# Two-block transformer on one core: the last four pairs of the second block's gates as seven block products, and the memory's norm and rounding beside the mixing's output product

## The reference, cut to what matters

```python
proj = h @ w_in[l]                      # h: 512 x 1024, the normed stream
q_a, k_a, v_a, u_b, gate_b, gate_c, g_a, g_b = jnp.split(proj, split_points, axis=-1)
...
branch_a = o_a @ w_branch_a[l]          # 512 x 512 @ 512 x 1024
branch_b = y_b @ w_branch_b[l]
merged = jax.nn.sigmoid(g_a) * branch_a + jax.nn.sigmoid(g_b) * branch_b
x = x + merged @ w_mix_out[l]
x = x + memory_cross_attention(rms_norm(x, norm_mem_q[l]), rms_norm(mem, norm_mem_kv[l]),
                               w_mem_q[l], w_mem_kv[l], w_mem_o[l])
```

## Time and profile before

| what | value |
|---|---|
| median of 3 runs | 1548.49 us (1548.48 to 1548.87) |
| profiled execution, its own time | 1548.38 us |
| its span | 1546.6 us |
| granted TensorE clock over the span | 0.999 |
| PE busy | 1536.8 us (99%) |
| VectorE, ScalarE, GpSimd busy | 1055.0, 754.5, 69.1 us |
| DMA | 161.88 MB, mean 105 GB/s |

### The profile page before, as it was taken

One profiled execution on the slowest core, in us unless ns is written; L12 is line 12 of the kernel. 1 busy time (PEld: TensorE's weight loads), 2 busy tenths in 40 slices (PEclk: granted clock), 3 DMA queues, 4 the chain that ended last, 5 costly groups with the idle time before them and its releaser, 6 DMA issues.

```text
span 1546.6 us, 22323 instructions
## 1 busy us (share of the span) xinstructions
PE 1536.8 (99%) x8348; PEld 1330.0 (86%) x8348; DVE 1055.0 (68%) x1755; ACT 754.5 (49%) x1307; POOL 69.1 (4%) x60
## 2 busy tenths in 40 slices
PE   9999999999999999999999999999999999999998
PEld 7888888888899899888888888888888899989987
DVE  6776887768789575447777545555555899948735
ACT  5446677744457445444544334344444445524514
POOL 0000000020000000210000010020002000000002
PEclk9999999999999999999999999999999999999999
DMA  5333222332323233324351242334123333322322
GB/s 195 122 109 97 88 78 93 103 129 90 127 84 110 96 96 108 97 82 131 118 141 62 71 137 87 118 118 156 55 82 109 110 103 110 124 96 82 110 89 75
DMA packets 56235, 161.88 MB, mean 105 GB/s; under 512 B 7232, under 2 KB 8640, under 8 KB 56000
## 3 DMA queue, kind: packets, MB, share of 16 engines
q1 hardware_dynamic: 55504, 159.41, 31.7%
q0 software_dynamic: 320, 0.52, 0.2%
q10 hardware_dynamic: 304, 0.52, 0.1%
HBM read 148.89 MB, written 2.10 MB: 98 GB/s over the span
## 4 chain that ended last, share of the span: by engine, by line
PE 96%; DVE 2%; ACT 1%; issue 1%; DMA 1%; SPq 0%; DVEq 0%; ACTq 0%
PE G L1490 66%; PE TP L1490 10%; PE SC L1490 9%; PE O L1490 5%; PE M L1490 5%; PE TP L1946 1%; PE TP L1892 0%; DMA T<-QK 0%; DVE WL L2623 0%; DMA GN<-in_gains 0%; PE TP L1995 0%; ACT L2030 0%; SPq L1465 0%; ACT WH L2033 0%; DVE T L2917 0%
## 5 line engine op out<-in xcount | busy, mean ns | idle before, releaser
L1490 PE MATMUL G<-XGh,WH 128*128 128x512 f32 x920 | 362.2, 394 | 0.0
L2623 DVE TENSOR_TENSOR WL<-RAW,WH 128x1024 fp32r<-128x1024 f32 (+2 forms) x269 | 282.7, 1055 | 116.5 <-ACT WH L2033 116.2
L1490 PE MATMUL G<-XGh,WL 128*128 128x512 f32 x920 | 358.4, 390 | 0.0
L1490 PE MATMUL G<-XGl,WH 128*128 128x512 f32 x920 | 358.3, 389 | 0.0
L2033 ACT ACTIVATE WH<-RAW 128x1024 fp32r<-128x1024 f32 (+2 forms) x275 | 240.0, 881 | 93.3 <-PE G L1490 60.8
L1490 PEld LDWEIGHTS G<-XGh,WL 128*128 128x128 f32 x920 | 172.7, 188 | 36.5
L1490 PEld LDWEIGHTS G<-XGh,WH 128*128 128x128 f32 x920 | 172.8, 188 | 36.1
L1490 PEld LDWEIGHTS G<-XGl,WH 128*128 128x128 f32 x920 | 172.9, 188 | 34.3 <-DVE XGl L2623 0.2
L1490 PE MATMUL G<-MGh,WH 128*128 128x512 f32 x372 | 145.0, 390 | 0.0
L1490 PE MATMUL G<-MGl,WH 128*128 128x512 f32 x372 | 144.8, 389 | 0.0
L1490 PE MATMUL G<-MGh,WL 128*128 128x512 f32 x372 | 144.7, 389 | 0.0
(11 more groups left out here) (443 smaller groups left out, 3268.8 us busy)
## 6 DMA issues: line engine op xcount, KB each, us to landing
RAW<-in_dn SPq DMA_DIRECT2D x30, 512.0 KB, 3.3
RAW<-in_fg SPq DMA_DIRECT2D x22, 512.0 KB, 4.2
RAW<-in_up SPq DMA_DIRECT2D x20, 512.0 KB, 3.4
RAW<-in_g SPq DMA_DIRECT2D x16, 512.0 KB, 3.4
RAW<-in_f SPq DMA_DIRECT2D x14, 512.0 KB, 3.7
X<-in_x SPq DMA_DIRECT2D x16, 256.0 KB, 4.3
RAW<-in_q SPq DMA_DIRECT2D x8, 512.0 KB, 3.3
RAW<-in_k SPq DMA_DIRECT2D x8, 512.0 KB, 3.4
```

What stands on the lines that cost most here:

```text
L1490: return e.matmul(dst, st, mv, start=start, stop=stop, skip_group_check=True)
L2623: return e.tensor_tensor(dst, src, hi.bitcast(F32), ALU.subtract)
```

## The change

A third section of seven block products is added: pairs `GATED + n` for n = 4 to 7, whose two units are `sa` n and `sb` n. Their left operands are made by `prepare_gates` during n = 0 to 3 from the rounded stream `XGh` + `XGl` into `QK`, `Vh`, `Vl`; the three unsummed ones are read from `XGh` and `XGl` themselves. The quarters are written to `RB` and `MSK` and pass a sigmoid there. `bb` and `ba` of n = 4 to 7 are given the thirds 0, 1, 0, 1 of `RAW`. The memory is loaded after pair 5, and its squares, norm and roundings are put beside the `mx` units.

```diff
+GATED, GATE_FIRST = MID + 20, 4
-RAW_MLP = {("up", 0): ..., ("dn", 8): PLACES, ("dn", 16): (0, 3, 0, 0, 2, 1, 0, 2),
+RAW_MLP = {("up", 0): ..., ("dn", 8): PLACES, ("bb", GATE_FIRST): (0, 1, 0, 1), ("ba", GATE_FIRST): (0, 1, 0, 1), ("dn", 16): ...
...
     for n in range(2, 8):
-        u += [("sa", n, 1024), ("sb", n, 1024), ("bb", n, 512), ("ba", n, 512)]
+        if n < GATE_FIRST:
+            u += [("sa", n, 1024), ("sb", n, 1024)]
+        else:
+            u += sevens(GATED - MID + n, GATED - MID + n + 1)
+        u += [("bb", n, 512), ("ba", n, 512)]
...
+    def prepare_gates(self, start):
+
+        for kt in range(4):
+            for n, kinds in enumerate((("h",), ("s13", "s2"), ("s4", "s_hi"), ("s_lo",))):
+                for kind in kinds:
+                    self.later(start + 3 * kt + n, kind, 2, kt)
+
+    def seven_gates(self, i):
+
+        f = GATED + i
+        for j in range(7):
+            self.tick()
+            if j == 0:
+                for n, kind in ((3, "one_out"), (3, "w_less"), (3, "v_less"), (4, "c22"), (5, "c11"), (6, "c12"), (6, "c21")):
+                    self.later(n, kind, f)
+                self.later(6, "sigmoid", f, 1)
+                self.later(7, "sigmoid", f, 0)
+            self.put("seventh", f, j, self.take("su", (f - MID, j)))
...
         self.drain()
+        self.prepare_gates(0)
         for n in range(2):
             branch(n, 0)
             self.put("merge_b", n)
-        self.put("mem_load")
-        for k in range(8):
-            self.later(4 + k, "sq", "mem", k)
-            self.later(20 + k, "mem_split", k)
-        self.later(17, "norm", "mem")
         for n in range(2, 8):
-            gates(n)
+            if n < GATE_FIRST:
+                gates(n)
+            else:
+                self.seven_gates(n)
+            if n == GATE_FIRST + 1:
+                self.put("mem_load")
             branch(n, 1)
             branch(n, 0)
             self.put("merge_b", n)
         self.drain()
 
     def memory(self):
+        for k in range(8):
+            self.later(k // 3, "sq", "mem", k)
+            self.later(8 + k, "mem_split", k)
+        self.later(5, "norm", "mem")
...
         def pair_source(f):
 
+            if f >= GATED:
+                return a["sa"][f - GATED], a["sb"][f - GATED]
...
+        def made_in(f):
+
+            return (RB[:, :], MSK[:, :]) if f >= GATED else (T[:, f % 2, :], T[:, 2 + f % 2, :])
...
+                elif kind == "sigmoid":
+                    f, w = arg
+                    table(ACT.Sigmoid)
+                    e.wait_ge(seven_dve, SEVEN_DVE["c12" if w else "c21", f])
+                    part = made_in(f)[1] if w else made_in(f)[0][:, HALF_S:S]
+                    e.activation(part, part, ACT.Sigmoid).then_inc(seven_act, 1)
```

More of the change, by code:

```diff
@@ L1302, in program @@
         PREP_ACT, PREP_DVE = tally("s_hi", "a_hi"), tally("h", "s13", "s2", "s4", "s_lo", "a_lo")
-        SEVEN_ACT, SEVEN_DVE = tally("one_out", "c11", "silu"), tally("w_less", "v_less", "c22", "c12", "c21")
+        SEVEN_ACT, SEVEN_DVE = tally("one_out", "c11", "silu", "sigmoid"), tally("w_less", "v_less", "c22", "c12", "c21")
         TURN7 = {f: k for k, f in enumerate(pairs)}
@@ L1369, in _ @@
                         e.wait_ge(prep_dve, PREP_DVE["s_lo", 0, 3])
+                    elif name == "sums" and f == GATED + GATE_FIRST:
+                        e.wait_ge(tb_done, TB["turn_b", 3, 2])
+                    elif name == "sums" and f == GATED + GATE_FIRST + 1:
+                        e.wait_ge(mb_lo, MB["merge_b", 2])
                     if behind:
@@ L1677, in _ @@
                     mid = f >= MID
-                    first, second = (f == pair for pair in first_pairs[0 if mid else 1])
+                    gated = f >= GATED
+                    first, second = (f == pair for pair in first_pairs[2 if gated else 0 if mid else 1])
                     wh, wl = w_tile(q) if mid else item_tile(q)
@@ L1681, in _ @@
                     bank = bank[:, 0:HALF_S]
-                    if j == 0:
+                    if gated and (j == 0 and (first or second)):
+                        e.wait_ge(ob_lo, PVB["pv_b", 3])
+                    elif gated and first and j in (1, 3):
+                        e.wait_ge(wtb_lo, 2 * 16)
+                    elif gated and (j == 2 and (first or second)):
+                        e.wait_ge(sb_win, 12)
+                    elif j == 0:
                         if first and mid:
@@ L1720, in _ @@
                         at = slice(kt * P, (kt + 1) * P)
-                        hi, lo = left_of[j](kt)
-                        if first and j in (0, 2):
+                        hi, lo = left_of_gates(j, kt) if gated else left_of[j](kt)
+                        if gated and first and j == 0:
+                            e.wait_ge(prep_dve, PREP_DVE["s_lo", 2, kt])
+                        elif first and j in (0, 2) and not gated:
                             e.wait_ge(prep_dve, PREP_DVE["s_lo" if j == 0 else "a_lo", 0 if mid else 1, kt])
@@ L2124, in _ @@
                             e.wait_ge(mb_lo, MB["merge_b", 7])
+                            e.wait_ge(w_lo, unit("su", (last_gated - MID, 6)))
+                            e.wait_ge(seven_dve, SEVEN_DVE["c21", last_gated])
                         elif name == "ffn":
@@ L3202, in _ @@
                     b, n = b_tiles(f), TURN7[f]
-                    first = f in (first_pairs[0][0], first_pairs[1][0])
-                    section = 0 if f >= MID else 1
+                    first = f in [pair[0] for pair in first_pairs]
+                    section = 2 if f >= GATED else 0 if f >= MID else 1
                     if not first and i in (1, 3):
@@ L3208, in _ @@
                         e.wait_ge(*lo_made)
+                    elif i == 1 and section == 2:
+                        e.wait_ge(mb_lo, MB["merge_b", 1])
                     elif i == 1:
```

120 lines of the change are left out of this document (86 added, 34 removed).

## The result

The changed kernel takes **1585.58 us** (median of four runs, 1583.64 to 1586.72) against 1548.49 us before, a ratio of 1.0238 with a 95% interval of 1.022 to 1.0256: 37 us slower. 1565.6 us was forecast, with a range up to 1573. The profiled execution took 1583.64 us and spans 1581.9 us, 35.3 us more than before.

A forecast was written before the change was run, and what follows sets the result against it. PE, busy 99%, was taken as the bound. Start 6.1, three periods of 21.0 and a tail of 13.4 make 82.5 us against 65.3 before: +17.2, so 1565.6 us, range 1556 to 1573.

The forecast's parts named there:

- Costed at nothing: Preparation beside plain gates' products, memory's part beside `mx`, its load and the sigmoids: all taken as hidden, 0 us.
- the start: From the end of `ba` 3 to the load of `bb` 4: 6.1 us, with 3.7 and 8 as ends.
- step 3: Next pair's transfers queue behind `bb` and `ba` on SyncE; the last lands 10.15 us after `bb`'s issue, ends 8.7 and 10.5.
- PE as the bound: PE is busy 99%; seven smaller products save 0.81 us per gate pair, 3.2 us for four, if PE never waits.
- Step 1 and 2: `one_out` waits on ScalarE behind `bb`'s rounding, so PE's fifth product starts about 3.6 us after `bb`'s load is issued.
- L: The moment SyncE issues the load of `bb` of pair n, from which one period's times are counted.
- Step 4: VectorE's chain from pair n + 1's first sum to its seventh operand's rest, 10.84 us; period 21.0 us.
- Step 5: PE stands 5.5 us before each pair's fifth product, once per period; 3.9 us for pair 4.
- The clock's rival: PE's clock falls to 1.2 GHz after each pause, adding 4.3 us behind the last: 1569.9 us, chance 0.15.

The follow-up runs named there:

- x13: The changed kernel with `gate_b(3, 1)` put ahead of the roundings of pair 4's first four operands on ScalarE: 1585.38 us.
- x12: The kernel before with the memory's part moved beside `mx`, its splits in pairs of multiplications with their rests a tick later: 1549.5 us.
- x4: The kernel before with the memory's part alone moved beside `mx`, plain gates kept, no preparation: 1557.14 us.
- x15: The changed kernel with the fourth product of pairs 5 to 7 repeated four times to fill PE's pause: 1583.88 us.
- x8: The changed kernel with the fourth product of pairs 5 to 7 repeated three times to fill PE's pause: 1582.99 us.
- x9: The changed kernel with next pair's transfers before `bb`, `bb`'s rounding after `one_out`, preparation and memory splits spread over ticks, `gate_b(3, 1)` before pair 4's roundings: 1569.04 us.

## Why the prediction was wrong

1565.6 us was forecast and 1585.58 measured, 20.0 more. Two steps failed. "Costed at nothing" put the memory's part and the preparation at 0 us where they cost 8.6 and 2.4. And for the pairs, whose loop was the one laid out, the start, the landing of step 3 and the clock behind the last pause were each taken too low: 4.2, 3.7 and 1.6 us by the marks of the profiled execution, some of it the preparation's, beside the 8.9 us that the medians leave for them.

**PE as the bound, 3.2 us to gain.** Right as far as it goes: a product of 256 took 0.120 us where the clock was full (1.44 us for twelve). None of it could be had.

**Step 1 and 2, `one_out` behind `bb`'s rounding.** Right. From the last load of `bb` to the fifth product it is 3.5 us (3.6 forecast), and ScalarE is named as releaser four times. ScalarE itself waited 3.9 to 4.1 us for each load of `bb`, not 2.6.

**Step 3, the landing.** Right in kind, low in size. From the load of `bb` to the first sum it is 10.96, 10.55 and 12.1 us; 10.15 was taken, with 10.5 as the high end, and all three lie above it. The issue was right (the transfer goes out at L + 5.4, forecast 5.3), the landing was 5.5, 5.1 and 6.5 us instead of 4.85. Over three periods that is 3.2 us more than 10.15 each, of the 3.7 that the periods were too long. What made the third so long stays open: nothing but its own pair's transfers and `ba` 6 went out just ahead of it, as with the others.

**Step 4, VectorE's row.** Right: 11.04 us from first sum to the next load of `bb`, three times over, 10.91 forecast.

**Step 5, the pause.** Right in place, rough in size: 5.5 us forecast three times, 6.1, 4.3 and 4.6 found, although each period was longer than laid out. The slow products behind a pause (1.75 us more than at the full clock behind the last) take up time in which PE would else stand before the next, so the shorter pauses are in part the clock's doing and no merit of the sum. For pair 4 it was 1.35 us instead of 3.9, since 3.7 us had been spent a little earlier, as x13 shows.

**The start.** The step that failed is "rest from 911.35 to 912.05": the rest of `bb` 3 stood at 914.37. Rows of VectorE in the changed kernel, the merge's rest of n = 2 first:

```profile
909.71 0.69 DVE L2713 TENSOR_TENSOR QK<-F,QK 128x512 fp32r<-128x512 f32 x1 [0.70 <-ACT QK L2097]
910.31 0.42 DVE L3367 TENSOR_TENSOR T<-T 128x256 f32<-128x256 f32 x1
911.95 0.69 DVE L2713 TENSOR_TENSOR QK<-T,QK 128x512 fp32r<-128x512 f32 x1 [1.22 <-ACT Vh L2097]
...
914.37 0.68 DVE L2713 TENSOR_TENSOR WL<-RAW,WH 128x512 fp32r<-128x512 f32 x1
```

I had left that merge's rest at 906.72, where the earlier trace rows have it; behind the preparation's first steps it stands at 909.71, and the last sum of kt 2 at 910.31 instead of 907.3. The load so left at 915.14, 3.0 us later than laid out, and `bb` 4's 4.2 us later. Of the other 1.2 us, 0.5 passed before the first sum, which stands behind the rest of `ba` 3 on VectorE (918.99 us), and 0.7 in VectorE's row, where it waited 0.5 us for the product of `ba` 3, slow behind the wait for `MSK`.

**The clock's rival** was real and had a chance of 0.15: products behind the pauses come at 1.2 GHz, and among the pairs only the last pause costs time, +1.6 us where +4.3 was priced, since not all three products were slow. It should have been part of the forecast. What it did not foresee is the same fall among `km`'s products, part of the 8.3 us.

**"Costed at nothing"** is the largest part of the miss. The preparation costs 2.4 us and the memory's part 8.6 us. I compared sums of busy time ("23.69 of 43.50 us", "eight `mem_split` bring 8 x 1.4 us"): by them there was room, and x12 shows that there is. But a `mem_split` of 1.4 us with its hand-over was laid beside a unit of 5.4 us without laying out the unit's own row, as step 4 had done for the pairs. Done so, x4's row is 7.5 us per unit against 5.44 of PE's, and by the time `km` begins PE has to wait 4.8 us in three waits, behind which products come at half the clock. The check that the prediction itself named, "among the `mx` units (the memory's part not hidden)", came true a little further on: PE's waits lie before `km`'s products, right behind the `mx` units.

In sum, of 37.1 us: 26.1 from the pairs, where 17.2 was forecast (with a delay of the start by the preparation in it) and the mechanism held, 8.6 from the memory's part, 2.4 from the preparation.

## What to carry to other kernels

Work that is put beside another stage is hidden by its order, not by its sum: lay out the whole row of the engine over one unit, hand-overs and all, and see that it is no longer than the unit, or by no more than the banks can cover. A step whose engine waits for the answer to its own last result costs the round trip each time; put the second half one tick later and fill the gap with the next one's first half. And where a loop runs over a shared buffer, a transfer and a long row of VectorE, count every link before moving one: taking one wait away only showed the next, four times here.

## What was not expected of the hardware

- A VectorE instruction with its inputs in SBUF that starts just behind the start of GpSimd's addition (1.33 us) ends only after it: 1.51 us for a scaling of 128x256 that takes 0.48 otherwise. GpSimd ends at 1026.95 in the rows of x4, the scaling at 1027.23. Half of the eight scalings of x4 are slow (about 480 ns or 1510 and more; in the kernel before all take 476 to 480), and in x12 the rests that stand there instead (1.85 us for two, 0.42 each otherwise). The Trainium skill, "SBUF — State Buffer", section "Who interferes with whom", says that a VectorE instruction with two SBUF inputs and a GpSimd instruction that reads SBUF exclude each other, the second to issue waiting in full; the trace agrees for the rests and the scalings, whose two inputs both lie in SBUF. The rest `XGl` that had begun 0.56 us before GpSimd was not slowed (0.75 us); whether GpSimd's addition waits in its turn, no row here shows, since it takes 1.33 us each time.
- The clock stayed at 1.00 behind pauses of 1.35 us (the change, pair 4), 1.4 us (x15) and 1.4 and 1.2 us (x8), and fell to about half behind each of the change's pauses of 3.7 us and more. In between it went either way: in x8 it fell behind 1.8 and 2.15 us, in x4 behind the third of three close waits of 1.7, 1.0 and 2.1 us, and in x9, where PE waits 13 times between 922 and 1020 us, once for 2.4 us, it read 1.00 all the way. The length of a pause alone does not say it.
